# PEER value rows of a two-layer encoder: 960 columns streamed whole through TensorE with scattered weights, 1088 gathered and added by VectorE

## The reference, cut to what matters

```python
def peer_ffn(xn, w_query, sub_keys, u, v):
    q = (xn @ w_query).reshape(b, s, PEER_HEADS, 2, PEER_DKEY // 2)
    sc = jnp.einsum('bshpc,hpnc->bshpn', q, sub_keys)
    s_top, i_top = lax.top_k(sc, 16)
    ...                                   # 16 best of the 16*16 sums of the two halves
    expert = jnp.take_along_axis(cand_idx, pos, axis=-1)   # 0..16383 = 128*key1 + key2
    gate = jax.nn.softmax(best, axis=-1)
    act = gelu(einsum('tkd,td->tk', u[expert], x))          # 8 heads * 16 experts a token
    return einsum('tk,tkd->td', gate * act, v[expert])
```

## Time and profile before

| | |
|---|---|
| median of 3 runs | 3296.12 us (3293.11 to 3303.31) |
| profiled execution: span | 3290.1 us |
| VectorE busy | 1604.4 us (49%) |
| TensorE matmul busy | 2676.2 us (81%) |
| GpSimd busy | 1152.3 us (35%) |
| HBM read | 1189.40 MB |
| of it gathers (queue q0) | 1073.81 MB |

### The profile page before, as it was taken

The page is one execution under the profiler, slowest core; times in us unless marked ns, Lnnn a source line. Parts: engine busy times, 40 slices in busy tenths (PEclk is TensorE's granted clock), DMA queues, the critical chain, the costliest instruction groups (busy, mean ns, idle before and its releaser), DMA issues. The chain is left out here.

```text
span 3290.1 us, 23740 instructions
## 1 busy us (share of the span) xinstructions
PE 2676.2 (81%) x7452; PEld 1314.1 (40%) x7452; DVE 1604.4 (49%) x2559; ACT 395.7 (12%) x923; POOL 1152.3 (35%) x1028
## 2 busy tenths in 40 slices
PE   8999996888888777777778867988887777777777
PEld 4685643544444323222223345444443232222223
DVE  1341216765555644444444367655566444444442
ACT  1241201110111101000001101011111010000001
POOL 0000003344454534443343124444445443333332
PEclk9999998999999999999999988999999999999999
DMA  5333246999999999999999959999999999999998
GB/s 221 128 115 141 103 191 232 384 415 421 420 391 405 410 427 408 427 427 428 428 427 427 360 221 371 416 425 418 394 398 406 427 412 427 427 428 427 427 427 311
DMA packets 157622, 1192.65 MB, mean 363 GB/s; under 512 B 17760, under 2 KB 18144, under 8 KB 18912
## 3 DMA queue, kind: packets, MB, share of 16 engines
q0 software_dynamic: 147456, 1073.81, 78.8%
q1 hardware_dynamic: 10080, 117.76, 8.9%
HBM read 1189.40 MB, written 2.10 MB: 362 GB/s over the span
## 5 line engine op out<-in xcount | busy, mean ns | idle before, releaser
L1467 PE MATMUL bank<-arena 128*128 128x512 f32 x4032 | 1865.0, 609 | 481.4 <-DMA arena<-pv,idxV 419.2
L1003 DVE CUSTOM_DVE_ANT_0 arena<-arena 128x2048 f32<-128x2048 f32 x512 | 1169.3, 2291 | 994.3 <-DMA arena<-pu,idxU 990.3
L1467 PEld LDWEIGHTS bank<-arena 128*128 128x128 f32 x4032 | 742.9, 192 | 1579.8 <-issue 978.1
L359 POOL DMA_INDIRECT arena<-pv,idxV x512 | 540.8, 1056 | 1159.7 <-PE bank L1467 997.9
L359 POOL DMA_INDIRECT arena<-pu,idxU x512 | 611.3, 1194 | 956.4 <-DVE idxU L998 590.0
L603 ACT ACTIVATE arena<-cst,arena 128x128 f32<-128x128 f32 x504 | 188.4, 397 | 1365.2 <-PE bank L1467 1242.7
L1424 PE MATMUL bank<-xnT,arena 128*128 128x256 f32 (+1 forms) x1280 | 229.3, 341 | 17.3 <-DMA arena<-wq 13.7
L1424 PEld LDWEIGHTS bank<-xnT,arena 128*128 128x128 f32 x1280 | 206.5, 194 | 44.6 <-DMA arena<-wq 14.5
L1179 PE MATMUL bank<-arena,xnT 128*128 128x512 f32 x448 | 198.4, 599 | 2.0 <-ACT xnT L430 0.8
L1179 PEld LDWEIGHTS bank<-arena,xnT 128*128 128x128 f32 x448 | 84.2, 192 | 101.6 <-issue 99.7
L1264 PE MATMUL bank<-xnT,arena 128*128 128x256 f32 x512 | 114.1, 379 | 0.7 <-issue 0.7
(11 more groups left out here) (190 smaller groups left out, 983.5 us busy)
## 6 DMA issues: line engine op xcount, KB each, us to landing
arena<-w_proj SPq DMA_DIRECT2D x22, 2048.0 KB, 7.5
arena<-wq SPq DMA_DIRECT2D x16, 2048.0 KB, 18.4
arena<-w_out SPq DMA_DIRECT2D x9, 2048.0 KB, 7.4
arena<-pu,idxU POOLq DMA_INDIRECT x512, 16.2
arena<-pv,idxV POOLq DMA_INDIRECT x512, 15.0
gB<-gains SPq DMA_DIRECT2D x5, 1024.0 KB
arena<-pool_w SPq DMA_DIRECT2D x1, 4096.0 KB, 12.1
h<-x SPq DMA_DIRECT2D x2, 1024.0 KB, 7.4
```

The lines of the kernel that those rows point to most:

```text
L359: nc.gpsimd.indirect_dma_start(ring[:, k % R], None, table[L], bass.IndirectOffsetOnAxis(idx[par][:, k:k + 1], 0)).then_inc(got[k % R], 16)
L1003: vec.tensor_tensor_reduce(out=u, in0=u, in1=xn, scale=1.0, scalar=0.0, op0=ALU.mult, op1=ALU.add, accum_out=act[:, par, k:k + 1]).then_in ...
L1467: ins = mm(psum[n][:, :], diag[:, k % DR], V[:, k % VR, n * BANK:(n + 1) * BANK], start=False, stop=bool(last) and k == (PK - 2 if last == ...
```

## The change

The columns of V are split. Columns 960 to 2047 (`VG` = 1088) are still gathered row by row, but VectorE adds them: one `scalar_tensor_tensor` of 128x1088, h += weight * row. Columns 0 to 959 (`VD`) are not gathered. All 16384 rows of them are read in order, as 128 blocks of 128x960 (`pvd`, laid out by second key), and multiplied on TensorE with a matrix W of 128 first keys x 128 tokens x 128 second keys for each block of tokens, zero but for each token's 128 weights. W is built by one-hot matrices: for every token a 128x128 matmul of onehot(key1) with onehot(key2)*weight. For block 0 ScalarE makes the one-hots, while the dots of block 1 run; for block 1 VectorE makes them, after the last dot.

The order changes too. All 256 U gathers and dots of a layer come first, then all V work. The V ring has seven slots: three in `xnT`, four where `U` and the arena were. So V's slots come free only when U's work is over. SyncE issues the 128 dense loads (480 KiB each, four slots). The pooling mixer of layer 1 no longer does block 0 early, and its matrices are loaded when V's work is over. Hardware loops are unrolled, and a wait before a gather is a wait of the DMA instruction's own, without the separate semaphore instruction (`hold`).

```diff
-UR, VR = 4, 4
-DR = 4
+UR = 4
+VD, VG = 960, D - 960
+VR, DR = 7, 4
...
             for L in range(LAYERS):
+                for n in range(ROWS):
+                    gather_u(L, n)
+                for m in range(ROWS):
+                    gather_v(L, m)
...
+            def gather_u(L, n):
+                g, k = n // PK, n % PK
+                if n >= UR:
+                    pool.wait_ge(s["dot_done"], L * ROWS + n - UR + 1)
...
+            def gather_v(L, m):
+                t, hk = m % TB, m // TB
+                if m >= VR:
+                    pool.wait_ge(s["vacc_done"], L * ROWS + m - VR + 1)
+                elif m >= 3:
+                    pool.wait_ge(s["dot_done"], (L + 1) * ROWS)
+                else:
+                    pool.wait_ge(s["q_mm"], (L + 1) * EVENTS)
...
+            def add_v(L, m):
...
+                vec.scalar_tensor_tensor(acc, vslots[m % VR], wv[:, t, hk:hk + 1], acc, ALU.mult, ALU.add
+                                         ).then_inc(s["vacc_done"], 1)
+            def one_hots(L, q):
...
+                vec.tensor_tensor(goh1[:, b], iota.unsqueeze(1).to_broadcast([P, QT, P]),
+                                  sT[:, 0, ts].unsqueeze(2).to_broadcast([P, QT, P]), ALU.is_equal)
+                for i in range(QT):
+                    ins = vec.tensor_scalar(goh2[:, b, i], iota, sT[:, 1, t:t + 1], sT[:, 2, t:t + 1], ALU.is_equal, ALU.mult)
...
+                weigh(L, 1)
+                for q in range(QUADS):
+                    one_hots(L, q)
+                    if q >= 1:
+                        add_v(L, done)
+                        done += 1
+                for m in range(done, ROWS):
+                    add_v(L, m)
+                add_dense(L)
...
+                if n >= DR:
+                    sp.wait_ge(s["vd_used"], L * (NK - 1) + n - DR + 1)
+                else:
+                    sp.wait_ge(s["dot_done"], (L + 1) * ROWS)
+                sp.dma_start(vdense[:, n % DR], pvd[L][n]).then_inc(vd_got[n % DR], 16)
...
+                pe.wait_ge(vd_got[n % DR], L * 16 * NK // DR + landed(n, DR))
+                for t in range(TB):
+                    for c in range(2):
+                        ins = mm(psum[2 * t + c][:, 0:VH], W[t][:, :, n], vdense[:, n % DR, c * VH:(c + 1) * VH],
+                                 start=n == 0, stop=n == NK - 1)
```

More of the change, by code:

```diff
@@ L210, in hybrid_encoder, with landed, event @@
         v_got = [ctx.enter_context(nc.semaphore(f"v_got{i}")) for i in range(VR)]
-        def hold(eng, name, value, passed):
-            eng.wait_ge(s[name], value)
-            eng.sem_inc(s[passed], 1)
+        vd_got = [ctx.enter_context(nc.semaphore(f"vd_got{i}")) for i in range(DR)]
+        def landed(m, ring):
+            return 16 * (m // ring + 1)
+        def event(t, hd):
+            return 2 * t + hd if hd < 2 else hd + 2
         class Steps:
             def __init__(self):
-                self.base, self.n = 0, 0
+                self.n = 0
             def link(self, eng, ins):
@@ L350, in _ @@
         def _(pool):
-            def gather(L, g, par, k, first, ring, R, table, idx, used, listed, got):
-                if L or not first or k >= R:
-                    hold(pool, used, L * ROWS + g * PK + k - R + 1, "pool_passed")
+            def gather_u(L, n):
+                g, k = n // PK, n % PK
+                if n >= UR:
+                    pool.wait_ge(s["dot_done"], L * ROWS + n - UR + 1)
+                elif L:
+                    pool.wait_ge(s["py_mm"], 4 + n + 1)
                 if k == 0:
-                    hold(pool, listed, L * GROUPS + g + 1, "pool_passed")
+                    pool.wait_ge(s["idx_ready"], L * EVENTS + event(g // PH, g % PH) + 1)
@@ L1065, in add_pooled, with add_dense @@
+            def add_dense(L):
+                v.wait_ge(s["dense_done"], L + 1)
+                for t in range(TB):
+                    for c in range(2):
+                        hv = h[:, t, c * VH:(c + 1) * VH]
+                        vec.tensor_tensor(hv, psum[2 * t + c][:, 0:VH], hv, ALU.add).then_inc(s["acc_evac"], 1)
             def add_pooled(t):
@@ L1154, in _ @@
+                weigh(L, 1)
+                done = 0
+                for q in range(QUADS):
+                    one_hots(L, q)
+                    if q >= 1:
[4 more added lines that the diff above has]
+                add_dense(L)
+            for t in range(TB):
+                norm(4, t)
         @block.tensor
@@ new lines, in spread @@
+            def spread(L, t, q):
+                n = QUADS * t + q
+                o1, o2 = (oh1, oh2) if t == 0 else (goh1, goh2)
+                pe.wait_ge(s["hot_dve" if t else "hot_act"], QUADS * L + q + 1)
+                if n >= 2:
+                    pe.wait_ge(s["spread_ev"], TB * QUADS * L + n - 1)
+                for i in range(QT):
+                    ins = mm(psum[4 + q % 2][:, i * P:(i + 1) * P], o1[:, q % 2, i], o2[:, q % 2, i], start=True, stop=True)
+                ins.then_inc(s["spread_mm"], 1)
@@ new lines, in _ @@
+                    for t in range(TB):
+                        pe.wait_ge(s["xn_ready"], 4 + t + 1)
+                        for n in range(KC // 2):
+                            for i in range(2):
+                                c = 2 * n + i
+                                ins = mm(psum[n][:, i * S:(i + 1) * S], xns[t][:, c * P:(c + 1) * P], PM[:, c // 4, t],
+                                         start=t == 0 and i == 0, stop=t == 1 and i == 1)
+                            if t:
+                                ins.then_inc(s["pool_mm"], 1)
```

621 lines of the change are left out of this document (251 added, 370 removed).

## The result

The changed kernel takes 3411.75 us (median of 4 runs, 3391.91 to 3428.78) where the kernel before takes 3295.87 (4 runs, 3293.11 to 3303.31): a ratio of 1.0349, 95% interval 1.0309 to 1.039. The profiled execution is the fastest of the four: 3391.91 us, a span of 3390.0. The forecast was 3380 us, with a range of 3215 to 3500, and 65% on slower. A ratio leaves out runs that took over 1.5% longer than the fastest of the same kernel; medians and ranges hold all runs.

The account below looks back on a forecast made before the run. The kernel before was held DMA-bound in PEER, chains of small work binding its ends. Terms 524 + 6 + 851 + 535 + 60 + 6 + 848 + 535 + 13.5 made a 3378 us span, forecast 3380, range 3215 to 3500.

Parts of the forecast that it names:

- U work, groups 0 to 6: Groups with routing, where VectorE was taken as the limit: 419 us in layer 0, dots 2.21 us apart plus routing events.
- U work, groups 7 to 15: The 144 dots a layer without routing: 3.0 us a dot, 432 us (354 to 467).
- V work until the dense part: From last dot to first dense matmul: 4 us, then 32 one-hot quads at 2.6 us on VectorE, 87 us.
- V work in all: One layer's V stage: 87 us, then 430 for 183.4 MB at 427 GB/s, plus 18; 535 us (520 to 590).
- seam: Last V add to the next layer's first U issue: 56 us before, 4 more for norms and block 0's pooling, 60.
- The ring: U gathers alone: four slots, late issue and 7.4 us latency give a 12.8 us loop, so U work is ring-bound there.
- My sign of 11.5 to 13 us a burst: Sign of a right forecast: in U work without routing, dots come in bursts of four, 11.5 to 13 us each.
- The bound of 3.24: Upper bound in us a dot without routing, seen in the earlier kernel's first group of layer 1.
- The lock: Two-SBUF-input VectorE instructions block GpSimd's U issues; without this the loop is 2.2 us shorter, the sum below 101 us lower.
- Rival 1: U ring keeps up: issue 0.94 us, groups 7 to 15 take 356 us instead of 432; total 3228 us; chance 0.25.
- Rival 2: Strided W loads bind TensorE in the dense part: three times 0.19 us a load, total 3650 us; chance 0.11.
- Rival 3: VectorE's adds starve POOL in V work beyond 2.0 us a row; at 2.2, V work 577, total 3464; chance 0.11.

## Why the prediction was right, and by what errors it came so near

The sum was 3378 us of span and the trace has 3390.0. That is nearer than the terms are, and to that extent it is luck:

| term | forecast | trace, layer 0 / layer 1 |
|---|---|---|
| first row | 6 | 7.8 / 5.8 |
| U work, groups 0 to 6 | 419 / 416 | 431.5 / 423.1 |
| U work, groups 7 to 15 | 432 | 408.6 / 395.1 |
| V work until the dense part | 87 | 95.1 / 95.1 |
| V work in all | 535 | 556.5 / 556.4 |
| seam | 60 | 68.1 |
| end | 13.5 | 13.5 |

U work came 11 and 30 us shorter than forecast, V work 21 us longer in each layer, the seam 8 longer: 41 us one way and 51 the other, which nearly cancel. What did not hang on luck is the direction: the bytes saved are given back by U work, which alone doesn't fill the DMA engines.

**The ring: right in kind, and its chain is there, but only for part of the rows.** The earlier trace rows gave a loop of 12.8 us with a held-up issue. A loop is the time from a dot to the fourth after it, which reads the same slot. At the end of layer 0 the changed kernel does just that. VectorE's and POOL's timeline, merged:

```profile
1353.79 2.29 DVE L1012 CUSTOM_DVE_ANT_0 arena<-arena 128x2048 f32<-128x2048 f32 x1 [2.78 <-DMA arena<-pu,idx_all]
...
1356.28 2.29 DVE L1012 CUSTOM_DVE_ANT_0 arena<-arena 128x2048 f32<-128x2048 f32 x1 [0.19 <-DMA arena<-pu,idx_all]
...
1356.36 3.02 POOL L392 DMA_INDIRECT arena<-pu,idx_all  x1 [3.31 <-DVE cst L1012]
...
1366.76 2.29 DVE L1012 CUSTOM_DVE_ANT_0 arena<-arena 128x2048 f32<-128x2048 f32 x1 [3.06 <-DMA arena<-pu,idx_all]
```

The slot freed by the dot of 1353.79 is asked for at 1356.36, the issue is held until 1359.38, 0.8 us after the next dot's end, and the row is used at 1366.76, 7.4 us later: 12.97 us a loop, with 338 GB/s moved in it. But elsewhere there is a second pattern, which no row of the kernel before showed:

```profile
2660.21 2.29 DVE L1012 CUSTOM_DVE_ANT_0 arena<-arena 128x2048 f32<-128x2048 f32 x1 [0.20 <-DMA arena<-pu,idx_all]
...
2663.61 2.22 POOL L392 DMA_INDIRECT arena<-pu,idx_all  x1 [0.30 <-issue]
...
2670.52 2.29 DVE L1012 CUSTOM_DVE_ANT_0 arena<-arena 128x2048 f32<-128x2048 f32 x1 [0.21 <-DMA arena<-pu,idx_all]
```

Here the dots stand evenly, every issue is held too (2.22 us), one follows the other without a pause, and the row is used 4.7 us after its issue ended: 10.31 us a loop, with 396 GB/s moved. The four-dot loops of groups 7 to 15 have a median of 11.07 us in layer 0 and 10.61 in layer 1; in an execution with half of the dense matmuls they had 12.28 and 10.45, and U work took 861 and 802 us. So a layer is a mixture: its loops run from 10.1 to 13.6 us, with many between the two shown, and the mixture differs from run to run. My sign of 11.5 to 13 us a burst holds for a part of them only. My 3.0 us a dot was mis-sized for this execution (2.84 and 2.74); over the seven profiled executions with four slots and these dots it is 2.64 to 3.14 a layer, 2.88 in the mean. The bound of 3.24 stands for one pattern. The mixture is also what spreads the changed kernel, 37 us over four runs. Four profiled executions of 3391.91, 3408.26, 3452.26 and 3444.97 us (the changed kernel twice, the wait in its own instruction, weights side by side) took 1658, 1671, 1716 and 1708 us of them in U work, and all that is left lies between 1733.7 and 1736.9, at the same mean granted clock of 0.742 to 0.746. With six slots, where the loop no longer decides, four runs lie within 11. What makes the ring leave one pattern for the other stays open. The argument of the prediction that a separate wait might bring "some tenths" was tried; nothing of it shows.

**The lock** was priced at 101 us, from 2.2 us a loop. With one factor in PSUM the gain was 91. The step holds, with its size.

**Groups 0 to 6** were under-priced by 7 to 12 us. Six slots show the bare VectorE time of a group with an event for both blocks, 50.7 us where I had 53 (groups 4 to 6 of layer 0 wait 0.2 us in all); the ring's waits there are 5 to 9 us a group, not 4.

**V work** was mis-sized in two terms. First, a quad takes 2.89 us and not 2.6. The 128-wide instructions follow each other every 0.26 us (four in 1.11), where I had about 0.2, and the terms that I wrote down (0.69, 0.8, 1.3) make 2.79 and not 2.6: a slip in the sum. So the dense part began at 95.1 and not at 87. Second, the rate: 410 GB/s, 4% under the 427 of the earlier trace rows, and so 447 us for the 183.4 MB and not 430. The 3% set aside covered part of it. That bytes bind there was right: half of the dense matmuls left V work at 558 to 562 us, and 4.2 MB less gave 8 to 10 us.

**The seam** measured 68.1 for 60: the pooling of block 0, which was done before under other work, now stands in it. With block 1's it is 64 matmuls, 15.9 us of the chain between last add and first issue, and 4 us was too little for that.

**The median.** I added 6 us to the span, after the kernel before. The profiled run here was the fastest of four, and the median stands 21.8 us above its span. This is the U ring's spread again, and it is why 3380 misses 3411.75 by 0.9% while the span is off by 0.4%.

**The rivals.** Rival 1 (the ring keeps up) was false for four slots as a whole, but the even pattern is its half-way house: 2.58 us a dot. As a remedy it was worth 142 us with one slot more and 170 with two. Rival 2 (strided weights) is refuted at its price: the load costs 0.10 us more, not 0.38, and hides. The Trainium skill's 16-byte lines (SBUF — State Buffer, Door 1: The DMA port swizzle) fit the direction; the factor seen here is 296 to 191. Rival 3 (adds starve POOL) didn't come about: in the dense stretch rows come every 2.19 us (300 us for 137), above its point of 2.0, but the DMA share is 1.03, and an issue lasts 0.93 us (127.89 for 137), so it is the blocks' share of the bytes that slows the rows, not POOL. My sign for it was VectorE idle for V rows with DMA below 400 GB/s; VectorE is idle and DMA stands at 410. The point itself was badly chosen: it compared the rows' pace with gathers alone.

## What to carry to other kernels

Before two streams that share a saturated DMA are put one after the other, ask of each alone whether its ring fills the DMA engines: slots times bytes over the loop from one use of a slot to the next. Here four slots of 1.05 MB over 10.3 to 13 us make 407 to 323 GB/s, and one slot more was worth 4% of the whole kernel. A buffer that is dead in the stage in question (here xnT and the room of the next stage's matrix) is the first place to look, and a gather ring that runs beside VectorE instructions with two SBUF inputs needs its issue time counted with them.

## What the runs showed of the hardware

- GpSimd's issue of a gather is held up while a VectorE instruction with two SBUF inputs runs: 2.2 us beside such dots, 949 ns beside dots of 2288 ns with one input in PSUM. The dots are not lengthened by the issues (2291 and 2288 ns).
- The same ring, under the same hold-up, ran with loops of 10.3 and of 13.0 us in one execution.
- Float32 weights with a stride of 512 bytes load in 296 ns, side by side in 191, both at the full granted clock. Under matmuls of 480 columns this cost nothing.
- With the DMA engines' share at 1.01 to 1.03 the rate was not everywhere the same: 427 GB/s in the kernel before, 417 with six U slots, 422 for rows of 8192 bytes beside whole-row adds, 410 for rows of 4352 bytes with blocks of 3840-byte rows, and 409 for both at 4096. That the length of the pieces is the reason was not tried by itself.
- A matmul stretch that is 99.9% busy was not the bound: with half of the work the stretch took as long, at the same 410 GB/s.
